# Turning activation tiles with VectorE 32x32 block transposes and a round trip through scratch memory, in place of TensorE and DMA transposes

## The reference

```python
# a hybrid layer, twice
p = rms_norm(x, norm_g) @ w_in            # qk, v, o, z_a, gates, xb, z_b
qk = silu(causal_dwconv(qk, qk_conv))     # convolution along time
y_a = norm(mlstm(q, k, v, i, f) * sigmoid(o)) * silu(z_a)
xc = causal_dwconv(xb, lru_conv_w) + b    # convolution along time
y_b = rg_lru(xc, w_a, w_x, lam) * silu(z_b)   # scan along time
x = x + concat([y_a, y_b]) @ w_out
# layers A, B, C, A
z = rms_norm(x, norm_g) @ w_in
q, k = rms_norm over each head            # then logits, softmax, @ v
x = x + concat([mix_out, mem_out]) * silu(gate) @ w_out
```

## Time and profile before

| | |
|---|---|
| time, median of 3 runs | 3274.63 us (3273.33 to 3274.72) |
| span of the profiled execution | 3271.3 us, 3.3 us under the median |
| PE busy | 3257.1 us (100%) |
| PEld busy | 2708.7 us (83%) |
| DVE busy | 2082.9 us (64%) |
| ACT busy | 1830.6 us (56%) |
| POOL busy | 174.0 us (5%) |
| DMA | 637.77 MB, mean 195 GB/s |

### The profile page before, as it was taken

The page is one execution under the profiler, slowest core; times in us unless marked ns, Lnnn a source line. Parts: engine busy times, 40 slices in busy tenths (PEclk is TensorE's granted clock), DMA queues, the critical chain, the costliest instruction groups (busy, mean ns, idle before and its releaser), DMA issues.

```text
span 3271.3 us, 39485 instructions
## 1 busy us (share of the span) xinstructions
PE 3257.1 (100%) x15142; PEld 2708.7 (83%) x15142; DVE 2082.9 (64%) x2843; ACT 1830.6 (56%) x2394; POOL 174.0 (5%) x241
## 2 busy tenths in 40 slices
PE   9999999999999999999999999999999999999999
PEld 7888888888888888888888888888888888888887
DVE  6558655756757755657667565665555667757664
ACT  5555545546665455546665565555556555565553
POOL 2000000000000000000000000000000321200000
PEclk9999999999999999999999999999999999999999
DMA  8666666565566666565567666556656565575565
GB/s 274 211 205 196 200 194 187 191 192 176 181 208 197 192 195 197 183 201 174 186 211 228 189 206 193 183 176 190 193 185 207 173 183 181 191 228 188 180 198 174
DMA packets 395740, 637.77 MB, mean 195 GB/s; under 512 B 102108, under 2 KB 104484, under 8 KB 395168
## 3 DMA queue, kind: packets, MB, share of 16 engines
q1 hardware_dynamic: 382928, 601.50, 59.2%
q0 software_dynamic: 10336, 27.45, 2.7%
q10 hardware_dynamic: 2288, 6.30, 0.5%
HBM read 608.10 MB, written 6.62 MB: 188 GB/s over the span
## 4 chain that ended last, share of the span: by engine, by line
PE 94%; ACT 2%; DVE 2%; DMA 1%; issue 1%; SPq 0%; ACTq 0%
PE acc L1727 29%; PE acc L1729 29%; PE acc L1728 29%; DVE weights_lo L1272 1%; PE tr L1814 1%; ACT weights_hi L946 1%; PE nm L1917 1%; ACT work L1012 1%; PE tr L1796 0%; PE tr L1727 0%; ACT work L1005 0%; PE tr L1729 0%; PE tr L1905 0%; PE tr L1728 0%; SPq L768 0%
## 5 line engine op out<-in xcount | busy, mean ns | idle before, releaser
L1272 DVE TENSOR_TENSOR weights_lo<-weights_raw,weights_hi 128x1024 fp32r<-128x1024 f32 x1103 | 1340.6, 1229 | 953.3 <-ACT weights_hi L946 950.0
L946 ACT ACTIVATE weights_hi<-weights_raw 128x1024 fp32r<-128x1024 f32 x1103 | 1156.0, 1057 | 1003.4 <-PE acc L1729 919.1
L1727 PE MATMUL acc<-weights_hi,u_hi 128*128 128x512 f32 x3136 | 1237.5, 395 | 0.0
L1729 PE MATMUL acc<-weights_hi,u_lo 128*128 128x512 f32 x3136 | 1222.6, 390 | 0.0
L1728 PE MATMUL acc<-weights_lo,u_hi 128*128 128x512 f32 x3136 | 1221.4, 389 | 0.0
L1727 PEld LDWEIGHTS acc<-weights_hi,u_hi 128*128 128x128 f32 x3136 | 588.9, 188 | 124.7 <-issue 4.0
L1729 PEld LDWEIGHTS acc<-weights_hi,u_lo 128*128 128x128 f32 x3136 | 588.5, 188 | 123.6
L1728 PEld LDWEIGHTS acc<-weights_lo,u_hi 128*128 128x128 f32 x3136 | 589.0, 188 | 119.3
L1727 PE MATMUL acc<-weights_hi,y_hi 128*128 128x512 f32 x1280 | 501.6, 392 | 0.9 <-DVE y_lo L1276 0.3
L1729 PE MATMUL acc<-weights_hi,y_lo 128*128 128x512 f32 x1280 | 498.6, 390 | 0.0
L1728 PE MATMUL acc<-weights_lo,y_hi 128*128 128x512 f32 x1280 | 498.2, 389 | 0.0
(11 more groups left out here) (285 smaller groups left out, 1957.7 us busy)
## 6 DMA issues: line engine op xcount, KB each, us to landing
weights_raw<-in_w_in_dram SPq DMA_DIRECT2D x384, 512.0 KB, 3.9
weights_raw<-in_w_out_dram SPq DMA_DIRECT2D x256, 512.0 KB, 4.4
weights_raw<-in_a_w_in_dram SPq DMA_DIRECT2D x176, 512.0 KB, 4.2
weights_raw<-in_b_w_in_dram SPq DMA_DIRECT2D x112, 512.0 KB, 3.7
weights_raw<-in_c_w_in_dram SPq DMA_DIRECT2D x112, 512.0 KB, 4.3
weights_raw<-in_w_mem_kv_dram SPq DMA_DIRECT2D x63, 512.0 KB, 5.1
kv_scratch<-work ACTq DMA_DIRECT2D x8, 512.0 KB, 5.3
qk_tiles<-in_w_a_dram POOLq DMA_DIRECT2D x8, 512.0 KB, 4.4
```

Of the source, the lines that this page charges most:

```text
L946: SC_E.activation(WH[:, b % RING], RAW[:, b % RING], ACT.Copy).then_inc(sem("hi_done"), 1)
L1272: V.tensor_tensor(WL[:, b % RING], RAW[:, b % RING], WH[:, b % RING].bitcast(F32), ALU.subtract).then_inc(sem("lo_done"), 1)
L1727: T.matmul(dst, hi_l, hi_r, start=start, stop=False, **kw)
L1729: return T.matmul(dst, lo_l, hi_r, start=False, stop=stop, **kw)
```

## The change

TensorE keeps 15 tiles of `tp`. The other 42 that it turned (20 `qt`, 10 `ct`, 8 `cz`, 4 `tp`) and all 39 of the DMA transposes now go another way, 81 tiles in all: `flip`, one VectorE instruction that transposes the 32x32 blocks of the tile; four stores by GpSimd's queue, 32 partitions each, to scratch in device memory; `fetch`, a load of 512 KB by SP that waits for the four stores; then `join` and `low`, `cjoin`, `qt` or `lrz`, which read the loaded tile in runs of 32. `fetch` stands ten slots behind `flip` in SP's list, the reader five slots behind it (eight for `lrz`). Convolution, gates of the recurrence and attention stand some slots later to make room.

```diff
-ISSUE, JOIN, LOW = 7, 5, 2
+FETCH, JOIN, LOW = 10, 5, 1
...
+    def turn(slot, src, ready, buf):
+        q = pl.piece(slot, "flip", src=src, ready=ready, buf=buf)
+        pl.piece(slot + FETCH, "fetch", at=q, buf=buf)
+        return q
+    def bounce(slot, src, ready, dst, kt0, gain, buf):
+        q = turn(slot, src, ready, buf)
+        p = pl.piece(slot + JOIN, "join", dst=dst, kt0=kt0, gain=gain, at=q, buf=buf)
+        pl.piece(slot + JOIN + LOW, "low", at=p, buf=buf)
+    def keys_in(hn, **kw):
+        q = turn(pl.here() + 1, "n", ("hn_out", hn), "n")
+        pl.piece(pl.here() + 6, "qt", at=q, buf="n", **kw)
...
-            pl.piece(pl.here() + 1, "ct", to="cx", at=cx)
+            q = turn(pl.here(), "xt", ("cx_x", cx), "x")
+            pl.piece(pl.here() + 5, "cjoin", at=q, buf="x")
...
-            c = pl.here() + 1
-            c += 4 if p == 0 else 2
+            c = pl.here() + 7
...
-            pl.piece(pl.here() + 3, "cz", at=zb)
-            pl.piece(pl.here() + 5, "lrz", l=l, p=p)
+            q = turn(pl.here(), "xt", ("zb_out", zb), "z")
+            pl.piece(pl.here() + 8, "lrz", l=l, p=p, at=q)
...
-                ts.append(attention(kind, grp, h - 3 if kind == "B" else h - 4))
+                ts.append(attention(kind, grp, h - 1))
...
+                    if p.kind == "fetch":
+                        sp.wait_ge(sem("spilled_" + LANE[p.buf]), 64 * (p.nth + 1))
+                        sp.dma_start(turned(p.buf), SPILL[LANE[p.buf]].rearrange("b r a e -> (b r) (a e)")
+                                     ).then_inc(sem("fetched_" + LANE[p.buf]), 16)
...
+                    if k == "flip":
+                        wait(pool, "flipped", p)
+                        for a in range(4):
+                            pool.dma_start(SPILL[LANE[p.buf]][:, :, a].rearrange("b r e -> r b e"),
+                                           flipped(p.buf)[32 * a:32 * a + 32].rearrange("p (b e) -> p b e", b=4)
+                                           ).then_inc(sem("spilled_" + LANE[p.buf]), 16)
...
+                        V.transpose(flipped(p.buf).rearrange("p (b q s) -> p q b s", b=4, q=8), src
+                                    ).then_inc(sem("flipped"), 1)
...
-                        for j in range(2):
-                            z = ZT[:, 2 * j:2 * j + 2]
-                            i = stt(z, z, 1.0, TR[:, j].rearrange("p (a b) -> p a b", b=256), ALU.add, ALU.mult)
+                        for t in range(2):
+                            for f in range(4):
+                                z = tokens(ZT, t)[:, f]
+                                i = stt(z, z, 1.0, by_token("z", t)[:, f], ALU.add, ALU.mult)
```

More of the change, by code:

```diff
@@ L1050, in _ @@
                         wait(act, "fc_ss", last.get("fc"))
+                        if last.get(("flip", "n")):
+                            act.wait_ge(sem("fetched_n"), 16 * (last["flip", "n"].nth + 1))
                         for t in range(2):
@@ L1087, in _ @@
                         wait(act, "gt_out", last.get("gt"))
-                        wait(act, "ct_pe", last.get("ct"))
-                        wait(act, "cz_pe", last.get("cz"))
-                        wait(act, "half_in", last.get("apart"))
+                        wait(act, "flipped", last.get("flip"))
                         for t in range(2):
@@ L1150, in _ @@
                         wait(act, "ge_o", last.get("ge"))
-                        wait(act, "ct_pe", last.get("ct"))
-                        wait(act, "cz_pe", last.get("cz"))
+                        wait(act, "flipped", last.get(("flip", "q")))
                         for t in range(2):
@@ L1229, in _ @@
                         wait(act, "gt_out", last.get("gt"))
-                        wait(act, "cz_pe", last.get("cz"))
+                        wait(act, "flipped", last.get(("flip", "z")))
                         for t in range(2):
@@ L1338, in _ @@
                                 i.then_inc(sem("tp_lo"), 1)
+                    elif k == "flip":
+                        ref(dve, p.ready)
+                        if p.nth:
+                            dve.wait_ge(sem("fetched_" + LANE[p.buf]), 16 * p.nth)
+                        if p.buf in ("q", "x"):
+                            wait(dve, "cj_out", last.get("cjoin"))
+                        elif p.buf == "z":
+                            wait(dve, "lrz_y", last.get("lrz"))
+                        elif p.buf == "n":
+                            wait(dve, "qt_out", last.get("qt"))
+                        else:
+                            wait(dve, "jn_lo", last.get(("low", p.buf)))
+                        if p.buf == "q":
+                            wait(dve, "mo_out", last.get("mo"))
+                            dve.wait_ge(sem("kv_st"), 16 * 8)
+                            dve.wait_ge(sem("tb_st"), 16)
+                        src = {"xt": XT, "o": O, "n": NBUF}.get(p.src)
+                        if src is None:
+                            src = X[:, :, CH * int(p.src[1]):CH * int(p.src[1]) + CH]
+                        V.transpose(flipped(p.buf).rearrange("p (b q s) -> p q b s", b=4, q=8), src
+                                    ).then_inc(sem("flipped"), 1)
                     elif k == "low":
@@ L1388, in _ @@
                         step(i)
-                        wait(dve, "qt_pe", last.get("qt"))
+                        wait(dve, "qt_out", last.get("qt"))
                         for t in range(2):
@@ L1396, in _ @@
                     elif k == "conv":
-                        if p.at:
-                            wait(dve, "cj_out", last["cjoin"])
-                        else:
-                            wait(dve, "ct_out", last["ct"])
+                        wait(dve, "cj_out", last["cjoin"])
                         if p.to == "cq":
@@ L1488, in _ @@
                         wait(dve, "gt_t", p)
+                        wait(dve, "fi_out", last.get("fi"))
                         for t in range(2):
@@ L1506, in _ @@
                             wait(dve, "tp_pe", last.get("tp"))
-                            wait(dve, "half_in", last.get("apart"))
+                            wait(dve, "flipped", last.get("flip"))
                         for t, ps in enumerate((NMB, SCB)):
@@ L1591, in _ @@
                         wait(dve, "tp_pe", last["tp"])
-                        wait(dve, "half_in", last["apart"])
+                        wait(dve, "flipped", last["flip"])
                         cs = slice(CH * p.j, CH * p.j + CH)
@@ L1652, in _ @@
                         wait(dve, "pv_out", last["pv"])
+                        if last.get(("flip", "n")):
+                            dve.wait_ge(sem("fetched_n"), 16 * (last["flip", "n"].nth + 1))
                         step(V.tensor_tensor(SQ, O, O, ALU.mult))
```

219 lines of the change are left out of this document (82 added, 137 removed).

## The result

| | before | after |
|---|---|---|
| time, median | 3274.47 us (3273.33 to 3274.72) | 3482.84 us (3480.03 to 3489.28) |
| ratio | | 1.0638 (1.0625 to 1.0651) |
| span of the profiled execution | 3271.3 us | 3479.0 us |
| mean granted clock | 1.000 | 0.977 |
| TensorE's waits, summed | 10.6 us | 174.3 us in 94 |

The change costs 6.4%: slower, as forecast, but by 208 us where 26 were forecast. The page of after, against the earlier trace rows: the granted clock by slice and the chain that ended last.

The account below looks back on a forecast made before the run. TensorE was taken to bound the kernel. Transposes saved 36.5 us; gates 7, recurrence 32 and 2, layer C 19, layers A and B 2 made +25.5 on the 3271.3 span, plus 3.3 to the median: 3300 us, range 3245 to 3338.

Parts of the forecast that it names:

- What bounds the kernel: TensorE, 94% of the chain, 2.73 us a slot; VectorE's `lo` may be about 6 us late before TensorE stalls.
- what goes: The 42 tiles of transposes leaving TensorE, at 0.87 us a tile: -36.5 us, all on the chain.
- VectorE's crowding: Flips, short gate instructions and pieces pushed together on VectorE make `lo` late, at the gates, recurrence and layer C.
- 7 for the gates: Gates of the two mLSTM layers: VectorE work filling three successive slots stalls 3.7 us each, +7 (6 to 9).
- 3.0 in p2 and p3: Recurrence, third and fourth quarters of each layer: scan, gate and flip share a slot, 3.0 us (2.8 to 4.0).
- 9.4 in layer C: Layer C, two groups of heads: VectorE's crowding makes `lo` late by 4.7 us a group.
- With a flip that ends at 3 to 5 us, the tile is there at 13 to 15: Times from the flip's slot start, taking 10.0 us from flip to loaded tile; ScalarE waits a microsecond or two.
- For the `join` tiles that is nothing. What costs are four places.: `hi` and `lo` have some 6 us to lose; costs only at mLSTM gates, recurrence, layer C, layers A and B.
- Terms 3 and 4: Layer C: crowding and late `qt` fetches, +19 (11 to 33); layers A and B: late `qt` fetches, +2 (0 to 9).
- The recurrence, 32 + 2: Two layers of four quarters: late `cjoin` delays `lgate`, +32 (17 to 47); each layer's last output, +2 (0 to 9).
- SP falls behind: Slower rival: fetches hold SP until four stores land, and weight loads queue behind; 3340 us or more, chance 10%.
- The route is hidden: Faster rival: tiles arrive 8.4 us after the flip, only VectorE's crowding stays; 3255 us (or 3267), chance 27%.

Follow-up runs that it names:

- e1: The changed kernel without the stores and loads, readers taking the flipped tile where VectorE wrote it (output not the reference's): 3286.91 us, 1.0032 of before.
- e12: The changed kernel with queries and keys back on TensorE, later readers, the recurrence's gate a slot behind the scan, and its own four stores and one load: 3324.48 us, 1.0142.
- e3: The changed kernel with readers one to three slots later where the plan has room, some loads two slots later: 3366.15 us, 1.0267.
- e6: The changed kernel with only queries and keys (20 tiles) back on TensorE, 61 tiles staying on the new way: 3415.85 us, 1.0433.
- e5: The kernel before, with VectorE making the same low part of the weights ten times more in 31 quiet slots: 3616.33 us, 1.1036.
- e2: The changed kernel with the load issued by GpSimd's queue behind its four stores, not by SP: 3549.87 us, 1.0834.
- e4: The kernel before, with VectorE making the same low part of the weights six times more in 31 quiet slots: 3442.59 us, 1.0515.

## Why the prediction was wrong

- **What bounds the kernel; what goes; VectorE's crowding.** Right. The cover of 6.0 measured 5.6, the flip 1.24 for 1.2. The terms that are crowding alone (7 for the gates, 3.0 in p2 and p3 of both layers, 2 for the last output, 9.4 in layer C: 30) stand against 35 us of waits in e1, and place by place they fit, but for the last output.
- **"With a flip that ends at 3 to 5 us, the tile is there at 13 to 15": the step that failed.** Both terms of that sum were too small. The way from the end of the flip, 10.0 us, measured 13.1 (10.9 to 18.2), near the upper bound of 13.5. The landing of the stores was taken as that of one store (3.0); four on one queue land one behind another, the last 4.6 after its issue. By the Trainium skill, "DMA: Bandwidth & Descriptors", section "Rules for kernel authors", transfers to disjoint halves of the partitions serialize; the rows agree, 8.4 us for four loads of 128 KB against 5.2 for one of 512. The Trainium skill's fit that the prediction worked out beside its sum ("DMA: Bandwidth & Descriptors", section "Anatomy of one DMA — SWDGE (gpsimd) path"), 2.3 us shorter, was further off still; the page gives it for DMAs that GpSimd issues, and the load is SP's. And the flip of a `join` tile ended 7.8 us after its slot began in the median, 4.9 at the least, since VectorE came to the flip behind other pieces. So these tiles were there at 20.9, not at 13 to 15.
- **"For the `join` tiles that is nothing. What costs are four places."** Wrong by these two terms: the reader waits not a microsecond or two but some 4 us at a place, 259 in all, past a cover that other pieces already use. Every kind of tile paid. With readers eight slots behind the flip (8 x 2.73 + 1.06 = 22.9 us) in place of five, the attention layers of e12 lost nothing, with their queries and keys on TensorE again.
- **Terms 3 and 4.** Mis-sized most: 21 us for the attention layers (19 + 2), of which a late query or key had 12, against 83 us of waits and 33 of lower clock, 101 net of saved transposes. In e1 12 of these 83 us stay, nearly all in layer C (3.7 twice among them); the others went with the way, so e1, e3 and e6 put them down to the late tiles. For layers A the plan was misread: `qt` and `lm` do not stand a slot apart there but in the same slot, and TensorE waited 5.7 and 5.4 us for them.
- **The recurrence, 32 + 2**: its place and mechanism (`lgate` behind a late `cjoin`) were right, and nearly the size: 15.0 us at `lgate` in six and 2.8 in each of p2 and p3, 26 in all; the last outputs had 7.9 for 2. What is missing in it is the last mLSTM tile (6.3 and 6.8 us) and the clock, 23 us of the +59.
- **The clock** was no term at all: 80.5 us of the account are neither waits nor transposes, 65 of them by the granted clock, and e5 shows 2.5 us lost behind a stall of 6.91.
- **The rivals.** "SP falls behind" gave 3340 or more and came nearest in time, and its sign showed (SP waits 165 us for stores), but its mechanism fell in e2: that it came nearest is luck. "The route is hidden" is nearly e1: 3287 against 3255 to 3267, higher by 14 us of clock and by 5 of waits.

## What to carry to other kernels

Price a transfer in pieces by when the last piece lands, and set the reader's distance from the end of its producer, not from its slot: a reader that stands in order on a busy engine holds up all that is behind it. Where TensorE is the bound, a stall can cost more than its length (1.5 to 3.0 us more at 59 of the 62 places of e4 and e5), so forecast stalls with the clock behind them. Taking work off a bounding engine wins nothing where the replacement lands on a chain without spare; look at the smallest idle time of that chain first.
